# Reordering the first loads of a decoder layer: weight chunk 0 goes between input tiles 1 and 2, chunk 1 between tiles 5 and 6

## The chip, the cores and the metric

The kernel runs on one core of one Trainium2 chip. The metric is the device time of one execution in microseconds (us); lower is better. A kernel's time is the median of several runs.

## What is computed

One post-norm decoder layer on 1024 tokens of width 1024, in float32. The part that matters here is the start of the first sublayer, where all projections read the same input:

```python
def hybrid_mixer(x, w_in, b_forget, conv_w, ...):
    z = x @ w_in                      # x: 1024 x 1024, w_in: 1024 x 4104
    q, k, v, f, glu_a, glu_g, sc_b, sc_c, sc_h = jnp.split(z, IN_SPLITS, axis=-1)
    ...                               # attention, two convolutions, gates, output projection
x = layer_norm(DEEPNORM_ALPHA * x + hybrid_mixer(x, ...), ln1_g, ln1_b)
x = layer_norm(DEEPNORM_ALPHA * x + grouped_moe(x, ...), ln2_g, ln2_b)   # 32 experts, top 2 of one group
```

## The kernel before

Every engine runs its own list of instructions, written out in program order, and waits on semaphores. An engine never passes an instruction that waits, so the order of each list is the order of the work.

**Products in three passes.** A float32 matrix is split into a rounded part `hi` and the rest `lo`; a product is `w_hi*x_hi + w_hi*x_lo + w_lo*x_hi`. ScalarE (ACT) makes each `hi` by a copy, VectorE (DVE) then makes `lo` by a subtraction, and TensorE (PE) multiplies (line 761).

**Input.** `x` comes in eight tiles of 128 tokens, 512 KB each (SyncE, line 393, one semaphore `tile_in[t]` a tile). TensorE transposes a tile with eight 128x128 transposes (line 778, `transpose_in(t)`) into a PSUM bank pair, ScalarE makes `xt_hi` (line 1183), VectorE `xt_lo` (line 1525). Tiles 4 to 7 take over the banks of tiles 1 to 4, so `transpose_in(4..7)` also waits for the VectorE split of tile 1, 2, 3, 4 (`xt_l`).

**Weights.** `w_in` comes in chunks of 512 rows by 128 columns, 256 KB each in pieces of 512 bytes (line 411, `raw(c)`), into a ring of four. Two chunks (the upper and the lower half of the rows) make one output tile of 128 columns by 1024 tokens. ScalarE splits a chunk in line 1179 (`hi_ok`), VectorE in line 1558 (`lo_ok`). `raw(c)` for c of 4 and more waits until the ring's slot is free; the first four wait for nothing.

**The head.** The first output tile is taken in halves, so that TensorE can begin before all of `x` is there: `first_pass(0)`, `(1)` and `(2)` are the three passes of chunk 0 over tokens 0 to 511 (four matmuls each: hi times hi, which waits for all four `xt_hi`; hi times lo, which waits for `xt_l` of 4; lo times hi, which waits for `lo_ok` of chunk 0). Then come `in_mm(1)` for the same tokens (12 matmuls, after chunk 1 is split) and both chunks for tokens 512 to 1023 (24 matmuls, after tile 7 is split). Four small transposes (line 815) follow, and from there the layer's projections run on, chunk after chunk.

The order of the lists before: SyncE issues x 0-3, chunk 0, chunk 1, x 4-7, chunk 2, chunk 3, then small parameters. ScalarE and VectorE split x 0-3, chunk 0, chunk 1, x 4-7, chunk 2 and so on. TensorE does transposes 0-3, `first_pass(0)`, `first_pass(1)`, transpose 4, `first_pass(2)`, transposes 5-7, `in_mm(1)`, the 24 matmuls.

Of the kernel before, what the change touches and what calls it, by code (L numbers as in the profile page):

```python
# [40 lines left out]
TT = SEQ // P  # L41
# [62 lines left out]
def program(nc, x, w_in, b_forget, conv_w, conv_b, conv_ln_g, conv_ln_b, sc_w,  # L104
# [12 lines left out]
    with ctx:  # L117
# [218 lines left out]
        def tiles(b, n=2):  # L336

            return ps[:, b:b + n, :].rearrange("p a (k n) -> p (a k) n", n=P)
# [23 lines left out]
        def x_bank(t):  # L362
            return (0, 2, 4, 6, 2, 4, 6, 2)[t]
# [26 lines left out]
        def _(sp):  # L390

            def load_x(t):
                sp.dma_start(x_raw[:, t, :], x[0, t * P:(t + 1) * P, :]).then_inc(tile_in[t], 16)

            def raw(c):

                if c < CB:
                    kind, half = KINDS[c % NCH // 2], c % 2
                    j = c // NCH
                    src = w_in[0, half * KC * P:(half + 1) * KC * P, j * P + COL[kind]:(j + 1) * P + COL[kind]]  # L400
                elif c < CC:
                    m, half = (c - CB) // 2, c % 2
                    src = w_gate[0, 1 + m // KT, half * KC * P:(half + 1) * KC * P, m % KT * P:(m % KT + 1) * P]
                else:
                    kind, j, half = STREAM[c - CC]
                    if kind == "g":
                        src = w_gate[0, 0, half * KC * P:(half + 1) * KC * P, j * P:(j + 1) * P]
                    else:
                        src = w_branch[0, j // KT, :, j % KT * P:(j % KT + 1) * P]
                sp.wait_ge(lo_ok, c + 1)  # L410
                sp.dma_start(w_raw[:, c % RING], src.rearrange("(k p) n -> p k n", p=P)).then_inc(raw_in[c % RING], 16)
# [12 lines left out]
                    sp.wait_ge(v_t, 2 * i)  # L424
                sp.dma_start(vt_raw[:], qkv_d[2, i * P:(i + 1) * P, :]).then_inc(v_in, 16)

            for t in range(4):
                load_x(t)
            raw(0)
            raw(1)  # L430
            for t in range(4, TT):
                load_x(t)
            raw(2)
            raw(3)
# [38 lines left out]
            for c in range(CC + 4, CE + 6):  # L473
# [10 lines left out]
                t = c - 5 - POS["b", KT, 0] + KT  # L484
# [269 lines left out]
        def _(pe):  # L754
            def product(o, terms, nk, cut, start, stop):


                for k in nk:
                    for n, (st, mv) in enumerate(terms):
                        for h, c0, c1 in cut:  # L760
                            last = nc.tensor.matmul(o(h, c1 - c0), st(k), mv(k, c0, c1),  # L761
                                                    start=start and k == nk[0] and n == 0,
                                                    stop=h in stop and k == nk[-1] and n == len(terms) - 1)
                return last
# [7 lines left out]
            def transpose_in(t):  # L772

                if t >= 4:
                    pe.wait_ge(xt_l, (2, 3, 4, 5)[t - 4])
                pe.wait_ge(tile_in[t], 16)
                for k in range(KT):
                    last = nc.tensor.transpose(tiles(x_bank(t))[:, k, :], x_raw[:, t, k * P:(k + 1) * P], ident[:])
                last.then_inc(xt_t, 1)
# [9 lines left out]
            def first_pass(n):  # L789

                w, v = ((w_hi, xt_hi), (w_hi, xt_lo), (w_lo, xt_hi))[n]
                product(lambda h, _: ps[:, h, :], [(lambda k: w[:, 0, k, :], lambda k, a, b: v[:, k, a:b])],
                        range(KC), HALVES[:1], n == 0, ())
# [6 lines left out]
            first_pass(0)  # L800
            pe.wait_ge(xt_l, 4)
            first_pass(1)
            transpose_in(4)
            pe.wait_ge(lo_ok, 1 + RING)
            first_pass(2)
            for t in range(5, TT):
                transpose_in(t)
            pe.wait_ge(lo_ok, 2 + RING)
# [25 lines left out]
            def scores(n):  # L834

                head, r = n // TT, ORDER[n % TT]
                u, nk, m0 = head % 2, ntiles(r) * P, r * P
                if n % TT == 0:
                    pe.wait_ge(qk_h, 3 * (head + 1))
                    pe.wait_ge(qk_l, 2 * (head + 1))  # L840
                    pe.wait_ge(aug_in[u], 32 * (head // 2 + 1))
                if n >= 2:
                    pe.wait_ge(exp_ok, n - 1)
                else:
                    pe.wait_ge(evac[n], 1 + CT * len(KINDS) // 2)
                out = s_bank(n)
                cut = [(h, a, min(a + HALF, nk)) for h, a in enumerate(range(0, nk, HALF))]
                product(lambda h, w: out[:, h * HALF:h * HALF + w],
                        [(lambda k, q=q: q[u][:, m0:m0 + P], lambda k, a, e, v=v: v[u][:, a:e])
                         for q, v in ((q_dup, k_two), (q_low, k_aug))],  # L850
                        [0], cut, True, [h for h, _, _ in cut if h != m0 // HALF])
                nc.tensor.matmul(out[:, m0:nk], ident_b[:], mask_b[:, 0:nk - m0],  # L852
                                 start=False, stop=True).then_inc(s_ok, 1)
# [34 lines left out]
            def gate_half(n):  # L888

                m, h, j = n // 4, n % 4 // 2, n % 2  # L890
                c = CB + 2 * m + j
                if h == 0:
                    pe.wait_ge(lo_ok, c + 1 + RING)
                if j == 0:
                    pe.wait_ge(tanh_ok, 2 * m + h + 1)
                last = product(lambda _, w: ps[:, 6 + h, :],
                               [(lambda k, w=w: w[:, c % RING, k - j * KC, :], lambda k, a, b, v=v: v[:, k, a:b])
                                for w, v in ((w_hi, xt_hi), (w_hi, xt_lo), (w_lo, xt_hi))],
                               range(j * KC, (j + 1) * KC), (HALVES[h],), j == 0, (h,) if j else ())
                if h == 1:  # L900
                    last.then_inc(w_used, 1)
                elif j == 1:
                    last.then_inc(g_mm, 1)
# [251 lines left out]
        def _(act):  # L1155
# [20 lines left out]
            def split_w(c):  # L1176
                act.wait_ge(raw_in[c % RING], 16 * (c // RING + 1))
                act.wait_ge(w_used, c + 1)
                nc.scalar.activation(w_hi[:, c % RING], w_raw[:, c % RING], ACT.Copy).then_inc(hi_ok, 1)  # L1179

            def split_x_in(t):
                act.wait_ge(xt_t, t + 1)
                nc.scalar.activation(xt_hi[:, :, t * P:(t + 1) * P], tiles(x_bank(t)), ACT.Copy).then_inc(xt_h, 1)  # L1183
# [25 lines left out]
                else:  # L1209
                    nc.scalar.activation(k_aug[u][0:DH, :], k_raw[0:DH, :], ACT.Copy).then_inc(qk_h, 1)  # L1210

            for t in range(4):
                split_x_in(t)
            split_w(0)
            split_w(1)
            for t in range(4, TT):
                split_x_in(t)
            for c in range(2, CB + 2):
                split_w(c)
# [272 lines left out]
        def _(dve):  # L1492
# [29 lines left out]
            def split_x_in(t):  # L1522
                dve.wait_ge(xt_h, t + 1)
                rows_ = slice(t * P, (t + 1) * P)
                nc.vector.tensor_tensor(xt_lo[:, :, rows_], tiles(x_bank(t)), xt_hi[:, :, rows_], ALU.subtract).then_inc(xt_l, 1)  # L1525
# [30 lines left out]
            def split_w(c):  # L1556
                dve.wait_ge(hi_ok, c + 1)
                nc.vector.tensor_tensor(w_lo[:, c % RING], w_raw[:, c % RING], w_hi[:, c % RING], ALU.subtract).then_inc(lo_ok, 1)  # L1558
# [12 lines left out]
                    f_link(nc.vector.tensor_tensor(f_lo[:], fc[:], f_hi[:], ALU.subtract))  # L1571
                    f_link(nc.vector.memset(fc[:], -1.0))

            for t in range(4):
                split_x_in(t)
            split_w(0)
            split_w(1)
            for t in range(4, TT):
                split_x_in(t)
            for i in range(CT):  # L1580
                link = Chain(conv_chain, i * CONV_LINKS)
# [456 lines left out]
```

## Time and profile before

| | |
|---|---|
| Median of 3 runs | 1656.99 us (1656.52 to 1657.79) |
| The profiled execution, its device time | 1657.7 us |
| Its span in the profile | 1656.0 us |
| TensorE busy in the span | 1589.0 us (96%) |
| TensorE's mean granted clock | 0.984 |

The span runs from the first to the last instruction of the profile; the device time holds 1.7 us more, which lie around it. Times in the profile are counted from the start of the span. The layer's first 28.8 us are the head described above; what follows, up to about 1000 us, is the mixer, and the experts stand behind that. "PE" is a matmul or transpose, "PEld" the load of its stationary operand.

### The profile page before, as it was taken

The numbers are of one execution on the slowest core, as the hardware profiler recorded it, in microseconds if no ns is written. First come the engines' busy times: TensorE is split into PE (matmuls) and PEld (weight loads), VectorE is DVE, ScalarE is ACT, GpSimd is POOL, SyncE is SP. The second block draws the span as 40 slices with busy tenths as digits, with TensorE's granted clock in tenths as the row PEclk, the third lists the DMA queues.
The fourth block names the chain that finished last, engine by engine and source line by source line (L and its number), as shares of the span: only waits on it lengthen the run. The fifth ranks groups of instructions, "written<-read, shape, count | busy, mean of one in ns | idle before, by whom it ended". The sixth has DMA issues, their size and how long they took to land.

```text
span 1656.0 us, 20267 instructions
## 1 busy us (share of the span) xinstructions
PE 1589.0 (96%) x7715; PEld 1314.2 (79%) x7715; DVE 1179.1 (71%) x1479; ACT 845.5 (51%) x1176; POOL 185.5 (11%) x219
## 2 busy tenths in 40 slices
PE   8999999999999999999999997999999999999981
PEld 6788888888888888888788885788888888888770
DVE  3756868585666666332575677799999999998884
ACT  3013211215655555325221334688888888888773
POOL 0000000202212220000000001111111111111120
PEclk9999999999999999999999998999999999999995
DMA  5153535644332321411554567999999999999966
GB/s 168 39 106 47 135 68 84 82 93 132 90 103 83 104 84 52 151 47 45 173 174 121 174 219 275 341 378 374 367 361 365 349 361 342 351 353 362 356 228 217
DMA packets 159065, 329.30 MB, mean 199 GB/s; under 512 B 17999, under 2 KB 87631, under 8 KB 158970
## 3 DMA queue, kind: packets, MB, share of 16 engines
q1 hardware_dynamic: 142826, 289.70, 54.1%
q0 software_dynamic: 16144, 38.32, 7.7%
q8 instruction: 61, 1.00, 0.2%
q14 instruction: 34, 0.28, 0.0%
HBM read 296.75 MB, written 48.52 MB: 208 GB/s over the span
## 4 chain that ended last, share of the span: by engine, by line
PE 88%; DMA 6%; DVE 4%; issue 1%; ACT 1%; SPq 0%; DVEq 0%; POOLq 0%; ACTq 0%
PE ps L761 53%; PE ps L1100 26%; DMA e_raw<-in_w_down 3%; PE ps L876 2%; PE ps L861 2%; DVE e_lo L1960 2%; DMA e_raw<-in_w_up 2%; PE ps L1107 1%; PE ps L1041 1%; DMA x_raw<-in_x 1%; PE ps L1113 1%; DVE zout L2020 1%; DVE zout L2013 1%; DMA z_d<-ye,row_i 0%; PE ps L1008 0%
## 5 line engine op out<-in xcount | busy, mean ns | idle before, releaser
L1960 DVE TENSOR_TENSOR e_lo<-e_raw,e_hi 128x1024 fp32r<-128x1024 f32 x376 | 436.1, 1220 | 24.9 <-ACT e_hi L1422 20.6
L1422 ACT ACTIVATE e_hi<-e_raw 128x1024 fp32r<-128x1024 f32 x376 | 367.5, 1050 | 22.2 <-DMA e_raw<-in_w_down 15.8
L761 PE MATMUL ps<-xt_hi,w_hi 128*128 128x512 f32 x896 | 302.3, 394 | 1.7 <-ACT w_hi L1179 1.7
L761 PE MATMUL ps<-xt_hi,w_lo 128*128 128x512 f32 x896 | 298.1, 390 | 0.0
L761 PE MATMUL ps<-xt_lo,w_hi 128*128 128x512 f32 x896 | 298.0, 390 | 0.0
L761 PEld LDWEIGHTS ps<-xt_hi,w_lo 128*128 128x128 f32 x896 | 168.1, 188 | 35.7
L761 PEld LDWEIGHTS ps<-xt_hi,w_hi 128*128 128x128 f32 x896 | 167.8, 188 | 34.7 <-ACT xt_hi L1183 1.9
L761 PEld LDWEIGHTS ps<-xt_lo,w_hi 128*128 128x128 f32 x896 | 168.4, 188 | 33.0 <-DVE xt_lo L1525 0.2
L1558 DVE TENSOR_TENSOR w_lo<-w_raw,w_hi 128x512 fp32r<-128x512 f32 x136 | 95.0, 703 | 131.9 <-ACT w_hi L1179 128.5
L1179 ACT ACTIVATE w_hi<-w_raw 128x512 fp32r<-128x512 f32 x136 | 83.8, 628 | 203.4 <-PE ps L761 195.5
L1100 PE MATMUL ps<-e_hi,xe_hi 128*128 128x512 f32 x512 | 163.6, 401 | 8.5 <-DVE e_lo L1960 7.9
L1100 PE MATMUL ps<-e_lo,xe_hi 128*128 128x512 f32 x512 | 159.6, 393 | 0.0
L1100 PE MATMUL ps<-e_hi,xe_lo 128*128 128x512 f32 x512 | 158.5, 391 | 0.0
L1598 DVE SCALAR_TENSOR_TENSOR conv<-upad,cols,conv 128x1024 f32<-128x1024 f32 x120 | 153.9, 1283 | 3.0
L1100 PEld LDWEIGHTS ps<-e_hi,xe_hi 128*128 128x128 f32 x512 | 92.4, 189 | 27.0 <-issue 8.5
L1100 PEld LDWEIGHTS ps<-e_hi,xe_lo 128*128 128x128 f32 x512 | 96.6, 189 | 21.5
L1100 PEld LDWEIGHTS ps<-e_lo,xe_hi 128*128 128x128 f32 x512 | 96.4, 188 | 21.2
L1245 ACT ACTIVATE pt_hi<-ps 128x1024 fp32r<-128x1024 f32 (+3 forms) x64 | 41.7, 652 | 113.5 <-PE ps L861 113.2
L1606 DVE TENSOR_REDUCE rmax<-ps 128x1 f32<-128x1024 f32 (+3 forms) x64 | 48.4, 756 | 67.7 <-PE ps L852 67.7
L1100 PE MATMUL ps<-e_hi,ht_hi 128*128 128x512 f32 x256 | 82.7, 404 | 3.7 <-DVE ht_lo L1972 3.3
L1100 PE MATMUL ps<-e_lo,ht_hi 128*128 128x512 f32 x256 | 80.1, 395 | 0.0
L1100 PE MATMUL ps<-e_hi,ht_lo 128*128 128x512 f32 x256 | 79.7, 393 | 0.0
(302 smaller groups left out, 2250.0 us busy)
## 6 DMA issues: line engine op xcount, KB each, us to landing
e_raw<-in_w_up SPq DMA_DIRECT2D x128, 1024.0 KB, 21.7
e_raw<-in_w_down SPq DMA_DIRECT2D x64, 1024.0 KB, 21.4
w_raw<-in_w_in SPq DMA_DIRECT2D x64, 256.0 KB, 4.9
w_raw<-in_w_gate SPq DMA_DIRECT2D x48, 256.0 KB, 3.3
gates_d<-gate_t POOLq DMA_DIRECT2D x16, 512.0 KB, 3.3
gate_s<-gates_d SPq DMA_DIRECT2D x16, 512.0 KB, 3.6
qkv_d<-qkv POOLq DMA_DIRECT2D x12, 512.0 KB, 3.7
w_raw<-in_w_branch SPq DMA_DIRECT2D x24, 256.0 KB, 3.7
```

The source lines that it names most:

```text
L761: last = nc.tensor.matmul(o(h, c1 - c0), st(k), mv(k, c0, c1), start=start and k == nk[0] and n == 0, stop=h in stop and k == nk[-1] and n ...
L861: last = nc.tensor.transpose(tiles(4)[:, k, :], prob[n % 2][:, k * P:(k + 1) * P], ident[:])
L876: last = nc.tensor.matmul(o_bank(j), v, p[n % 2][:, k, :], start=k == 0 and s == 0, stop=k == nk - 1 and s == 1)
L1041: last = nc.tensor.matmul(lg, x1t[:, k, :], w_rt[:, k, :], start=False, stop=k == KT - 1)
L1100: last = nc.tensor.matmul(ps[:, banks + h, :], st[:, s, :], w[:, s0 % RSPL, h * HALF:(h + 1) * HALF], start=s == 0 and m == 0, stop=s == n ...
L1179: nc.scalar.activation(w_hi[:, c % RING], w_raw[:, c % RING], ACT.Copy).then_inc(hi_ok, 1)
L1245: nc.scalar.activation(pt_hi[n % 2][:, 0:ntiles(r), (r % 2) * P:(r % 2 + 1) * P], tiles(4)[:, 0:ntiles(r), :], ACT.Copy).then_inc(pt_h, 1)
L1422: nc.scalar.activation(e_hi[:, (UPT + s) % RSPL, :], e_raw[r][:, s % 2, :], ACT.Copy).then_inc(e_h, 1)
L1558: nc.vector.tensor_tensor(w_lo[:, c % RING], w_raw[:, c % RING], w_hi[:, c % RING], ALU.subtract).then_inc(lo_ok, 1)
L1598: link(nc.vector.scalar_tensor_tensor(dst, upad[:, j:j + SEQ], col(ROW_CONVW + j, i), dst, ALU.mult, ALU.add))
L1606: nc.vector.tensor_reduce(rmax[:, n % 2:n % 2 + 1], s_bank(n)[:, 0:ntiles(ORDER[n % TT]) * P], AX.X, ALU.max, negate=True).then_inc(max_ok, 1)
L1960: nc.vector.tensor_tensor(e_lo[:, sp_, :], e_raw[raw_slot(b, s)][:, s % 2, :], e_hi[:, sp_, :], ALU.subtract).then_inc(e_all, 1)
```

## The change

The order of four lists is changed; no instruction is added or removed. SyncE issues x 0-1, chunk 0, x 2-5, chunk 1, x 6-7. ScalarE and VectorE split x 0-2, chunk 0, x 3-5, chunk 1, x 6-7. TensorE does `first_pass(2)` right behind `first_pass(1)`, and transpose 4 after it.

```diff
--- before.py
+++ after.py
@@ -424,11 +424,13 @@
                     sp.wait_ge(v_t, 2 * i)
                 sp.dma_start(vt_raw[:], qkv_d[2, i * P:(i + 1) * P, :]).then_inc(v_in, 16)
 
-            for t in range(4):
+            load_x(0)
+            load_x(1)
+            raw(0)
+            for t in range(2, 6):
                 load_x(t)
-            raw(0)
             raw(1)
-            for t in range(4, TT):
+            for t in range(6, TT):
                 load_x(t)
             raw(2)
             raw(3)
@@ -800,9 +802,9 @@
             first_pass(0)
             pe.wait_ge(xt_l, 4)
             first_pass(1)
-            transpose_in(4)
             pe.wait_ge(lo_ok, 1 + RING)
             first_pass(2)
+            transpose_in(4)
             for t in range(5, TT):
                 transpose_in(t)
             pe.wait_ge(lo_ok, 2 + RING)
@@ -1209,11 +1211,13 @@
                 else:
                     nc.scalar.activation(k_aug[u][0:DH, :], k_raw[0:DH, :], ACT.Copy).then_inc(qk_h, 1)
 
-            for t in range(4):
+            for t in range(3):
                 split_x_in(t)
             split_w(0)
+            for t in range(3, 6):
+                split_x_in(t)
             split_w(1)
-            for t in range(4, TT):
+            for t in range(6, TT):
                 split_x_in(t)
             for c in range(2, CB + 2):
                 split_w(c)
@@ -1571,11 +1575,13 @@
                     f_link(nc.vector.tensor_tensor(f_lo[:], fc[:], f_hi[:], ALU.subtract))
                     f_link(nc.vector.memset(fc[:], -1.0))
 
-            for t in range(4):
+            for t in range(3):
                 split_x_in(t)
             split_w(0)
+            for t in range(3, 6):
+                split_x_in(t)
             split_w(1)
-            for t in range(4, TT):
+            for t in range(6, TT):
                 split_x_in(t)
             for i in range(CT):
                 link = Chain(conv_chain, i * CONV_LINKS)
```

## Rows read from the trace of the kernel before

**Rows 1.** The chain that ended last: start us, us, what it was.

```profile
4.01 11.36 DMA x_raw<-in_x
20.40 8.38 PE ps L761 x36
29.15 349.50 PE ps L761 x1540
```

**Rows 2.** Busy us (instructions) of PE, PEld, DVE, ACT, POOL; clock, DMA share, GB/s.

```profile
0.00:28.80 28.80, 20.82 (x113) 17.25 (x114) 12.01 (x12) 12.84 (x14) 1.64 (x13) 1.00 0.54 189
...
1030.00:1480.00 450.00, 446.40 (x2117) 370.39 (x2116) 418.51 (x440) 366.14 (x420) 66.67 (x49) 1.00 0.98 359
```

**Rows 3.** TensorE in order of time: start us, us, what, [idle before <- releaser].

```profile
12.31 1.16 PE L761 MATMUL ps<-xt_hi,w_hi 128*128 128x512 f32 x4 [1.72 <-ACT w_hi L1179]
13.31 1.09 PE L761 MATMUL ps<-xt_lo,w_hi 128*128 128x512 f32 x4
15.50 1.06 PE L778 MATMUL ps<-ident,x_raw 128*128 128x128 f32 x8 [1.10 <-DMA x_raw<-in_x]
16.32 1.18 PE L761 MATMUL ps<-xt_hi,w_lo 128*128 128x512 f32 x4
17.34 3.06 PE L778 MATMUL ps<-ident,x_raw 128*128 128x128 f32 x24
20.16 0.47 PE L761 MATMUL ps<-xt_hi,w_hi 128*128 128x512 f32 x1
```

**Rows 4.** TensorE between 5.5 and 6.0 us, instructions begun or running then.

```profile
5.25 1.06 PE L778 MATMUL ps<-ident,x_raw 128*128 128x128 f32 x4
```

**Rows 5.** ScalarE (ACT) in order of time.

```profile
11.54 0.62 ACT L1179 ACTIVATE w_hi<-w_raw 128x512 fp32r<-128x512 f32 x1
...
16.60 1.03 ACT L1183 ACTIVATE xt_hi<-ps 128x1024 fp32r<-128x1024 f32 x1 [1.87 <-PE ps L778]
```

**Rows 6.** VectorE (DVE) in order of time.

```profile
9.66 3.49 DVE L1525 TENSOR_TENSOR xt_lo<-ps,xt_hi 128x1024 fp32r<-128x1024 f32 x3 [0.39 <-ACT xt_hi L1183]
13.07 0.68 DVE L1558 TENSOR_TENSOR w_lo<-w_raw,w_hi 128x512 fp32r<-128x512 f32 x1
...
19.47 3.49 DVE L1525 TENSOR_TENSOR xt_lo<-ps,xt_hi 128x1024 fp32r<-128x1024 f32 x3 [0.58 <-ACT xt_hi L1183]
```

**Rows 7.** SyncE issuing the first loads, in order of time.

```profile
0.92 1.82 SPq L393 DMA_DIRECT2D x_raw<-in_x  x4
2.79 1.18 SPq L411 DMA_DIRECT2D w_raw<-in_w_in  x2
```

**Rows 8.** Issue to landing: x 0-1, x 2-3, chunks 0-1, x 4-7, chunks 2-3.

```profile
DMA to landing us min/median/max: 4.0/4.4/4.8
...
DMA to landing us min/median/max: 6.2/6.7/7.1
...
DMA to landing us min/median/max: 7.3/9.0/10.7
...
L393 SPq DMA_DIRECT2D x_raw<-in_x x4: 457/700/1024, 4.0 to 6.3; - x4
...
DMA to landing us min/median/max: 11.4/11.8/12.9
...
L411 SPq DMA_DIRECT2D w_raw<-in_w_in x2: 1072/2033/2994, 7.1 to 8.2; - x2
...
DMA to landing us min/median/max: 13.4/14.6/15.7
```

**Rows 9.** DMA rate between 0 and 30 us, in slices of 0.75 us.

```profile
GB/s 0 0 87 300 251 399 361 284 366 426 360 310 125 55 125 131 236 343 424 426 409 400 382 315 160 118 98 55 30 24 28 32 29 31 16 4 34 48 90 246
```

**Rows 10.** Stretches before and after a fall of the clock; columns as in rows 2.

```profile
8.40:12.30 3.90, 2.14 (x18) 1.68 (x17) 3.51 (x4) 3.48 (x4) 0.00 (x0) 1.00 0.44 146
1044.00:1046.00 2.00, 0.64 (x3) 0.59 (x4) 2.00 (x3) 2.00 (x3) 0.00 (x0) 1.00 0.39 135
1046.00:1050.00 4.00, 4.00 (x12) 3.11 (x11) 4.00 (x5) 3.44 (x4) 0.00 (x0) 0.57 0.64 207
```

## Prediction, made before the changed kernel ran

> **What bounds the kernel now.** I read the chain that ended last first [rows 1]. It goes through the wait for an input tile, then TensorE from 20.40 us on, and from 29.15 us TensorE without a break for 349.50 us. So the change is worth what it moves the end of the head, and the reader should watch one number: E = 20.40 + 8.38 = 28.78 us, where the last of the first two chunks' matmuls ends. Behind E the order is the same. The mixer is TensorE's; in the experts, TensorE is busy 446.40 of 450 us with the DMA engines at a share of 0.98 [rows 2]. Their stream is started by the mixer's end, so I carry a shift of E to the end one to one.
>
> Second, TensorE in order of time [rows 3]. Of 28.8 us it is busy 20.82 [rows 2], so idle 8.0. About 5.0 of them pass before tile 0 has landed, 1.72 in the wait for chunk 0's `w_hi`, 1.10 in the wait for tile 4; the brackets show none from 15.50 on. So only some 3 us of idle time stand behind the first 5.0, and there is a little in the first transposes: four take 1.06 us at 5.25 [rows 4], eight take 1.06 at 15.50 [rows 3]. That stretch ran at the lower clock level, 1.2 GHz against 2.4. The whole head can thus give back some 3 to 4 us at most, if every wait went.
>
> Third, the lists that feed it [rows 5, 6]. VectorE splits a tile in 3.49/3 = 1.16 us and a chunk in 0.68; ScalarE takes 1.03 and 0.62. Fourth, the landings, issue [rows 7] plus time to landing [rows 8]: tiles 0 and 1 at 4.9 and 6.1, tiles 2 and 3 at 8.0 and 9.4, chunk 0 at 2.79 + 7.3 = 10.1, chunk 1 at 3.42 + 10.7 = 14.1, tile 4 at 4.01 + 11.4 = 15.4, tile 7 at 6.3 + 12.9 = 19.2, chunk 2 at 7.1 + 13.4 = 20.5, chunk 3 at 8.2 + 15.7 = 23.9. A tile takes 1.3 us of the stream and, at the same rate, a chunk 0.65. But chunk 1 took 4.0 behind chunk 0, and chunk 3 took 3.4 behind chunk 2; between 9 and 12 us the rate falls to 55 to 131 GB/s [rows 9]. Two chunks in a row starve the stream.
>
> **Part 1, TensorE: `first_pass(2)` ahead of transpose 4.** Chunk 0's `w_lo` was ready at 13.07 + 0.68 = 13.75, but its pass ran at 16.32, behind transpose 4, which waited for its landing. The move fills the 1.10 us of idle time with 0.95 us of work that came later. Alone it would be worth 0.9 to 1.0 us. The cover of tile 4's landing is then this pass.
>
> **Part 2, ScalarE and VectorE: chunk 0 ahead of tile 3.** `first_pass(1)` needs all four `xt_l`. Before, VectorE's run 9.66 + 3.49 = 13.15 ended it, and chunk 0 came after. Now chunk 0's 0.68 stands before tile 3 on VectorE, and its 0.62 before tile 3 on ScalarE, where `first_pass(0)` waits too. The same 0.68 us is on the path that sets the start of the second pass; the third pass no longer needs it.
>
> **Part 3, SyncE: chunk 0 ahead of tiles 2 and 3.** Tiles 0 and 1 are issued as before. Chunk 0 is issued at 1.84, and tiles 2 and 3 land later by what it costs. *Lower bound*: only its bytes, 0.65 us: tile 2 at 8.65, tile 3 at 10.05. *Upper bound*: chunk 1's row, 4.0 us behind tile 1's 6.1, and tiles 1.3 each after it as tile 4 behind chunk 1: chunk 0 at 10.1, tile 2 at 11.4, tile 3 at 12.7. The nearest row is chunk 0 behind tiles (0.7 after tile 3), but it had four tiles to hide behind and now has two, so I take twice the bytes, 1.3 us, an estimate: tile 2 at 9.3, tile 3 at 10.7. Chunk 1 has four tiles ahead of it, as chunk 0 had, and comes at 10.7 + 2.6 + 0.7 = 14.0 at the earliest, up to 19.3 by the 4.0 (15.3 for tile 5). Tile 7 comes by 19.2, since the same ten transfers ended then; up to 21.9 by the upper bound.
>
> **The path to T, the start of transpose 4.** Middle case: tile 2's transposes 9.4 to 10.35, ScalarE tile 2 to 11.5, chunk 0 to 12.15, tile 3 to 13.2; VectorE tile 2 from 11.55 to 12.7, chunk 0 to 13.4, tile 3 to 14.6. Passes two and three take 0.95 to 1.0 each [rows 3], so T = 14.65 + 1.95 = 16.6. With the lower bound VectorE ends tile 3 at 13.95 and T is 15.9. With the upper, tile 3 is transposed by 13.75, copied by 14.9, split by 16.15: T = 18.1. Before, T was 15.50, but with the third pass still ahead, so 16.45 is what to hold it against.
>
> **Part 4, ScalarE and VectorE: chunk 1 behind tile 5.** This one I charge in full. Before, chunk 1 landed at 14.1 and was split while TensorE waited, so `in_mm(1)` began at 20.16 straight behind the transposes. Now its split stands behind tiles 4 and 5, which are not even transposed before T: ScalarE begins tile 4 at T + 1.10 [rows 3, 5], ends it 1.03 later, and VectorE does tile 4, tile 5 and chunk 1 in 1.16 + 1.16 + 0.68 = 3.0. `in_mm(1)` begins at T + 2.15 + 3.0 = T + 5.15. The four tiles' transposes end at T + 4.0 (32 at 3.06/24), so TensorE waits about 1.1 us there. Tiles 6 and 7 are split by T + 7.5, before the 12 matmuls end at T + 7.9, so there is no wait behind them. The 36 matmuls took 28.78 - 20.16 = 8.62 us, with a wait for tile 7, whose split ended only at 22.96 [rows 6]; at 349.50/1540 = 0.227 us each [rows 1] and 0.2 for the end of the last they take 8.35. E = T + 13.5. Chunk 1's landing hides up to T + 3.1, and tile 7's up to E - 9.
>
> **Sum.** Lower bound: 15.9 + 13.5 = 29.4, +0.6 us. Middle: 16.6 + 13.5 = 30.1, **+1.3 us**. Upper: 18.1 + 13.5 = 31.6, +2.8 us. Against the profiled execution's 1657.7 that is 1659.0; the median is 0.7 lower, so the median becomes 1656.99 + 1.3 = **1658.3 us**. 0.2% is 3.3 us, about what a measurement of this kernel can tell from no change, and all three sums lie inside it. Chunks 2 to 5 keep their place: the next matmuls after E need chunk 2, which lands at 20.5.
>
> One rule is weighed against a row here. Chunk 1 landed 4.0 us behind chunk 0, with equal bytes. The Trainium skill, "DMA: Bandwidth & Descriptors", section "Anatomy of one DMA", states for DMAs issued from GpSimd a fixed 2.0 us plus bytes over 436 GB/s, and that many descriptors can be emitted before their cost shows. By it chunk 0 would cost 0.6 us of the stream, and the sum would be the lower bound, +0.6; the 4.0 us of the row speak against it, and the row decides.
>
> **Rivals.**
> *The gap closes.* The reorder gives what part 1 is worth and VectorE's list costs less than I charge: T = 13.15 + 1.95 = 15.1 and `in_mm(1)` follows the transposes at T + 4.7 as before, so E = 15.1 + 13.0 = 28.1 to 28.4, -0.5 us: 1656.5. For it: 1.10 us of idle time really goes. Against it: chunk 0 and chunk 1 both stand in front of splits that gate.
> *TensorE's clock falls in the head, slower.* Between 8.4 and 13.2 us TensorE would have only tiles 2 and 3 to transpose, some 2.1 us in 4.8 (a share of 0.44); before it was 2.14 in 3.90 (0.55), at full clock. In the experts' start it was busy 0.64 of 2.00 us, and the next 4 us were granted 0.57 [rows 10]. If the clock falls to 1.2 GHz there, the three passes and some transposes take twice as long for about such a stretch: +1.7 us more, 1660.0. It decides the sign by 0.2% only with the upper bound of part 3 beneath it: 2.8 + 1.7 = +4.5 us, 1661.5. The Trainium skill, "TensorE: Matmul & The Clock Gate", Part 1, has the idle array at 1.2 GHz and the busy one at 2.4; the trace agrees [rows 4, 10], and by it the time would be this rival's 1660.0.
> *Chunks starve the stream, slower.* As the upper bound, and worse: each chunk costs 4 us where it stands and nothing makes it up. From a landing of tile 3 later than about 13.2, or of tile 7 later than 23, E passes 32.1 and the time 1660.3, slower by over 0.2%. For it: both second chunks cost 3.4 and 4.0. Against it: both came behind another chunk, and here each comes behind tiles.
>
> **How the numbers follow.** The sum from lower to upper bound (1657.6 to 1659.8): 0.63. The gap closes (1656.5): 0.16. The clock falls (about 1660, a third of it beyond 0.2%): 0.12. Chunks starve the stream beyond the bound (over 1660.3): 0.06. More than 3.3 us gained, for which there is no idle time to find: 0.03. Faster 0.03, slower 0.06 + 0.04 = 0.10, within 0.2% 0.87. The range 1656.4 to 1660.2 holds the sum, the gap rival and most of the clock rival; some 0.15 is left out.
>
> **What would show it.** In the changed profile: tile 3's transposes near 10.8 (10.1 to 12.8); no idle time for tile 4 in front of T; VectorE ending tile 3's split near 14.6; `first_pass(1)` waiting for VectorE; T near 16.6; TensorE waiting about 1 us for chunk 1's `w_lo` near 21.7; E near 30.1; the continuous TensorE run after it as long as before. Wrong would be: E below 28.8, a clock under 1.00 between 9 and 25 us, tile 7 landing past 21, or a total that moves by other than E does.

## The result and the profile after

The changed kernel takes 1662.01 us (median of ten, 1660.11 to 1664.68), the kernel before 1657.80 (ten, 1655.97 to 1658.87). The ratio is 1.0028, interval 1.0020 to 1.0036: slower by 0.28%, where I had forecast +0.08%. It is outside the range, and on the side that I had given a chance of 0.10. A second measurement of the changed kernel (e12 below) gave 1.0026 (1.0017 to 1.0035). The forecast started from three executions of the kernel before; the ten lie 0.8 us higher, which is part of the distance to the forecast 1658.3 but not of the ratio. One of the twelve executions of a later experiment, e11, took 6589.92 us, and its ratio leaves that one out.

The chain that ended last in the changed kernel, its first 34 us, as in [rows 1]; start us, us, what:

```profile
2.86 9.37 DMA x_raw<-in_x
...
15.35 4.73 PE ps L763 x12
...
22.05 2.36 DVE xt_lo L1529 x2
24.41 0.61 DVE w_lo L1562
...
25.06 8.45 PE ps L763 x36
```

E, the end of the first two chunks' matmuls, is 25.06 + 8.45 = 33.51 us; before it was 28.78. That is +4.7 us in the profiled execution. The DMA in the first line is tile 3's load. Two later pieces of the same chain:

```profile
33.88 349.50 PE ps L763 x1540
...
804.55 111.81 PE ps L763 x492
```

The second of them in the kernel before:

```profile
799.81 111.81 PE ps L761 x492
```

The first is as long as in [rows 1] and 4.73 us later; the second, near the mixer's end, is as long as before and 4.74 us later. TensorE in order of time, to be held against [rows 3] (this kernel's line 763 is 761 there, 780 is 778):

```profile
11.02 1.10 PE L780 MATMUL ps<-ident,x_raw 128*128 128x128 f32 x8 [2.81 <-DMA x_raw<-in_x]
12.27 1.97 PE L780 MATMUL ps<-ident,x_raw 128*128 128x128 f32 x8 [0.15 <-DMA x_raw<-in_x]
15.35 2.07 PE L763 MATMUL ps<-xt_hi,w_hi 128*128 128x512 f32 x4 [1.11 <-ACT xt_hi L1185]
17.23 1.91 PE L763 MATMUL ps<-xt_lo,w_hi 128*128 128x512 f32 x4
18.93 1.15 PE L763 MATMUL ps<-xt_hi,w_lo 128*128 128x512 f32 x4
19.92 2.78 PE L780 MATMUL ps<-ident,x_raw 128*128 128x128 f32 x24
23.33 1.09 PE L780 MATMUL ps<-ident,x_raw 128*128 128x128 f32 x8 [0.63 <-DVE xt_lo L1529]
25.06 0.50 PE L763 MATMUL ps<-xt_hi,w_hi 128*128 128x512 f32 x1 [0.64 <-DVE w_lo L1562]
```

Two things are to be seen. Tile 2's transposes begin at 11.02, after 2.81 us of idle time, where they followed tile 1's without a gap before. And tile 3's eight transposes take 1.97 us and the first two passes 2.07 and 1.91, where eight transposes took 1.06 before and these passes 1.16 and 1.09 [rows 3]. The windows of the changed kernel, columns as in [rows 2], say why (the last three numbers are clock, DMA share, GB/s):

```profile
8.00:11.00 3.00, 0.21 (x1) 0.00 (x0) 2.04 (x2) 1.02 (x1) 0.00 (x0) 1.00 1.00 406
...
14.00:19.00 5.00, 3.89 (x11) 2.87 (x10) 2.26 (x3) 1.02 (x1) 0.00 (x0) 0.50 0.74 257
```

The granted clock is 0.50 between 14 and 19 us, that is 1.2 GHz, after a stretch in which TensorE was busy 0.21 of 3.00 us. The landings, in the form of [rows 8], for tiles 0-1, chunk 0, tiles 2-5, tiles 6-7:

```profile
L393 SPq DMA_DIRECT2D x_raw<-in_x x2: 397/408/420, 0.9 to 1.4; - x2
...
DMA to landing us min/median/max: 3.5/3.9/4.4
...
L411 SPq DMA_DIRECT2D w_raw<-in_w_in x1: 425/425/425, 1.8 to 1.8; - x1
...
DMA to landing us min/median/max: 7.8/7.8/7.8
...
L393 SPq DMA_DIRECT2D x_raw<-in_x x4: 446/511/2070, 2.3 to 3.9; - x4
...
DMA to landing us min/median/max: 8.7/9.7/10.9
...
L393 SPq DMA_DIRECT2D x_raw<-in_x x2: 512/690/867, 7.1 to 8.0; - x2
...
DMA to landing us min/median/max: 9.8/10.0/10.3
```

Tile 1 lands at 1.4 + 4.4 = 5.8, chunk 0 at 1.84 + 7.8 = 9.7, tile 2 at 2.31 + 8.7 = 11.0, tile 3 at 2.86 + 9.4 = 12.2, tile 7 at 8.0 + 10.3 = 18.3. Chunk 0 lands 3.9 us behind tile 1, and tiles 2 and 3 land 2.9 and 2.8 us later than the 8.0 and 9.4 of before, not 1.3. Yet the ten transfers end at 18.3, not later than the 19.2 of before.

How the chunk costs so much shows in the packets. DMA between 5.2 and 7.5 us, and between 7.5 and 9.7, in the changed kernel:

```profile
DMA packets 416, 0.25 MB, mean 110 GB/s; under 512 B 12, under 2 KB 403, under 8 KB 416
```

```profile
DMA packets 272, 0.85 MB, mean 385 GB/s; under 512 B 23, under 2 KB 71, under 8 KB 272
```

In the first stretch some 390 packets of 512 bytes move at 110 GB/s, and some 13 of 4 KB with them, at a DMA share of 0.53: the DMA engines are idle for nearly half of the stretch, so it is not the moving of the bytes that takes the time. In the second the stream is back at 385 GB/s with 201 packets of 4 KB, all of them of tile 2 and behind (tile 1 had landed at 5.8), and 48 of 512 bytes trickle in between; chunk 0 counts as landed only with the last of them, at 9.7. Tile 2 fares the same. A tile is 128 packets of 4 KB, so tile 2's are among the first 384. Up to its landing at 11.0 some 600 had begun, against some 490 up to its landing at 8.0 in the kernel before:

```profile
DMA packets 1192, 2.72 MB, mean 248 GB/s; under 512 B 80, under 2 KB 592, under 8 KB 1192
```

(1192 less the 592 small ones.) A landing waits for the last piece, while the other pieces of the stream run on. That is how tiles 2 and 3 come later and the last tile does not.

### The profile page after: what moved, and what is told of

It is laid out like the page before. It is cut to its first block, busy times and chain, and to the rows that moved or that the text cites. A ratio compares the mean times of both kernels' runs of the same rounds, so it can differ in the third digit from the quotient of the medians.

```text
span 1660.0 us, 20267 instructions
## 1 busy us (share of the span) xinstructions
PE 1593.6 (96%) x7715; PEld 1317.4 (79%) x7715; DVE 1178.9 (71%) x1479; ACT 845.0 (51%) x1176; POOL 185.8 (11%) x219
## 4 chain that ended last, share of the span: by engine, by line
PE 87%; DMA 6%; DVE 4%; issue 1%; ACT 1%; SPq 0%; DVEq 0%; POOLq 0%; ACTq 0%
PE ps L763 53%; PE ps L1102 26%; DMA e_raw<-in_w_down 3%; PE ps L878 2%; PE ps L863 2%; DVE e_lo L1966 2%; DMA e_raw<-in_w_up 2%; PE ps L1109 1%; PE ps L1043 1%; PE ps L1115 1%; DVE zout L2026 1%; DMA x_raw<-in_x 1%; DVE zout L2019 1%; PE ps L1010 0%; DMA z_d<-ye,row_i 0%
## 5 line engine op out<-in xcount | busy, mean ns | idle before, releaser
L1102 PEld LDWEIGHTS ps<-e_hi,xe_hi 128*128 128x128 f32 x512 | 92.5, 189 | 27.5 <-issue 9.1
L1102 PEld LDWEIGHTS ps<-e_hi,xe_lo 128*128 128x128 f32 x512 | 96.4, 188 | 21.5
## 6 DMA issues: line engine op xcount, KB each, us to landing
e_raw<-in_w_up SPq DMA_DIRECT2D x128, 1024.0 KB, 21.7
```

What stands on the lines that cost most here:

```text
L1102: last = nc.tensor.matmul(ps[:, banks + h, :], st[:, s, :], w[:, s0 % RSPL, h * HALF:(h + 1) * HALF], start=s == 0 and m == 0, stop=s == n ...
```

## The experiments

E is read from each trace's chain; T is the start of transpose 4, as in the prediction. In e2 and e3 TensorE keeps its old list, so the third pass still stands behind T, as in the kernel before (15.5). "Time" is the ratio to the kernel before in the same measurement, with its interval. An execution's time scatters by some 2 us around its median, and a trace's E is that of one execution. The traces of e6 and e8 are of the shortest of their executions, 3.9 and 4.0 us below the medians, so their E may be lower than usual.

| kernel | tile 3 lands | T | E | E against 28.78 | time |
|---|---|---|---|---|---|
| changed | 12.2 | 19.9 | 33.5 | +4.7 | 1.0028 (1.0020 to 1.0036) |
| e1, TensorE's list alone | 8.6 | 15.3 | 28.1 | -0.7 | 1.0000 (0.9991 to 1.0009) |
| e2, SyncE's list alone | 12.6 | 18.6 | 31.8 | +3.0 | 1.0025 (1.0014 to 1.0035) |
| e3, the splits' lists alone | 9.2 | 15.6 | 29.9 | +1.1 | 1.0004 (0.9995 to 1.0013) |
| e11, all but SyncE's list | 9.1 | 16.2 | 29.8 | +1.0 | 1.0004 (0.9995 to 1.0012) |
| e4, kept busy 20 + 12 | 12.5 | 20.5 | 34.2 | +5.4 | 1.0031 (1.0019 to 1.0042) |
| e9, kept busy 9 + 5 | 11.5 | 17.4 | 31.0 | +2.2 | 1.0031 (1.0019 to 1.0042) |
| e5, chunk 0 in 2 KB pieces | 10.7 | 17.5 | 31.1 | +2.3 | one run, 1656.3 us |
| e6, chunk 1 split early | 12.1 | 18.8 | 31.5 | +2.7 | 1.0027 (1.0018 to 1.0037) |
| e7, four tiles first | 9.0 | 15.7 | 28.9 | +0.1 | 1.0002 (0.9994 to 1.0011) |
| e8, chunks on a second queue | 12.3 | 19.2 | 32.0 | +3.2 | 1.0031 (1.0022 to 1.0041) |
| e10, chunk 0 ahead of all | 12.4 | 19.4 | 32.1 | +3.4 | 1.0020 (1.0012 to 1.0029) |
| e12, changed again | 13.0 | 21.5 | 35.2 | +6.4 | 1.0026 (1.0017 to 1.0035) |
| e13, kept busy 12 + 5 | 11.7 | 19.7 | 33.3 | +4.6 | 1.0019 (1.0010 to 1.0028) |
| e14, kept busy 9 + 5 again | 12.9 | 18.9 | 32.5 | +3.7 | one run, 1661.4 us |
| e15, changed, third trace | 12.4 | 20.5 | 34.1 | +5.4 | one run, 1662.8 us |

(Tile 0 landed between 4.4 and 4.9 in these traces, 4.9 in the kernel before; e10's landed at 8.4.)

**One list at a time.** e1 is the kernel before with

```diff
-            transpose_in(4)
             pe.wait_ge(lo_ok, 1 + RING)
             first_pass(2)
+            transpose_in(4)
```

> The kernel before with one edit: first_pass(2) ahead of transpose 4. E is the end of the first two chunks' matmuls, 28.78 us before. By part 1 of the prediction the pass fills the 1.10 us wait for tile 4, so E is 27.8 to 27.9 and the time 0.9 to 1.0 us less. The rival, read only now: tile 7 lands at 19.2 and its transposes began at 19.34, so the landing holds the transposes, the 36 matmuls begin at 20.2 either way and E stays at 28.7 to 28.9, time unchanged.

The rival holds. TensorE's rows of e1:

```profile
14.41 1.09 PE L761 MATMUL ps<-xt_hi,w_lo 128*128 128x512 f32 x4
15.34 1.98 PE L778 MATMUL ps<-ident,x_raw 128*128 128x128 f32 x16
17.54 1.06 PE L778 MATMUL ps<-ident,x_raw 128*128 128x128 f32 x8 [0.22 <-DMA x_raw<-in_x]
18.84 1.07 PE L778 MATMUL ps<-ident,x_raw 128*128 128x128 f32 x8 [0.23 <-DVE xt_lo L1525]
```

The pass runs at 14.41, the 1.10 us gap is gone, and TensorE then waits for tiles 6 and 7 as they land. Tiles 0 and 7 landed 0.5 us sooner in this trace, and E is 0.7 sooner. Counted from tile 7's landing, E comes after 28.11 - 18.70 = 9.4 us, before after 28.78 - 19.20 = 9.6. So part 1 of the prediction is worth at most some 0.2 us by itself; the time (1.0000, with 0.0009 on either side) could not tell 1 us from nothing.

e2 takes over only SyncE's part of the diff, e3 only the two split lists, e11 everything except SyncE's part.

> The kernel before with SyncE's new order alone (x 0-1, chunk 0, x 2-5, chunk 1, x 6-7); the splits and TensorE keep the old order. If the landings carry the loss, tile 2 lands near 11.0 and tile 3 near 12.3 as in the changed kernel, TensorE's clock falls to 1.2 GHz in the wait too, and E is 30.4 at full clock, 31.5 to 32.5 with the fall, +1.6 to +3.7 us. If the order of the splits carries it (rival), E stays below 29.5.

> The kernel before with the new order of ScalarE's and VectorE's splits alone; loads and TensorE as before. By parts 2 and 4 of the prediction the second pass waits 0.7 us longer and chunk 1's split behind tile 5 delays the 12 matmuls to about 21.4: E 29.8 to 30.0, +1.0 to +1.3 us, at full clock throughout. If the landings alone carry the loss (rival), E is 28.7 to 29.0 and the time unchanged.

> The changed kernel with SyncE's order of before (x 0-3, chunk 0, chunk 1, x 4-7): the new splits and the new place of first_pass(2) alone. By the prediction's parts 1, 2 and 4 with full-rate landings T is 15.5 to 15.9 and E 29.2 to 29.6, +0.5 to +0.9 us; what is left to the changed kernel's 33.4 is then SyncE's order with the fallen clock, 3.9 to 4.2 us. If the three lists only lose together (rival), E is 31 or more.

e2 has nearly the whole loss in the time (0.25 of 0.28%), with tile 2 landing at 11.3 and tile 3 at 12.6; of E it has 3.0 of the 4.7. The clock fell in it too, but only for the transposes of tiles 2 and 3 (16 in 3.58 us); its passes ran at full pace. e3 and e11 have E at 29.9 and 29.8, with all passes at full pace. e3's wait, which part 4 of the prediction charged:

```profile
17.41 3.08 PE L778 MATMUL ps<-ident,x_raw 128*128 128x128 f32 x24
21.42 0.50 PE L761 MATMUL ps<-xt_hi,w_hi 128*128 128x512 f32 x1 [0.92 <-DVE w_lo L1560]
```

The 12 matmuls begin at 21.42 behind chunk 1's `w_lo`, where I had written "about 21.4". T in e3 is 15.6 against 15.5 before, since tile 4's landing at 15.4 holds it in both; so the 1.1 us are part 4's, and part 2 costs nothing there. The lists of the splits cost 1.0 to 1.1 us of E and SyncE's list the rest. The times add up in the same way: 0.25% for e2 and 0.04% for e11, 0.28% for the changed kernel.

**What a chunk costs.** e5 reads chunk 0 as 128 rows of 2 KB in place of 512 pieces of 512 bytes. It leaves out the right weights of chunk 0, so that the first output tile holds other numbers:

```diff
+                if c == 0:
+                    sp.dma_start(w_raw[:, 0].rearrange("p k n -> p (k n)"), w_in[0, 0:P, 0:KC * P]).then_inc(raw_in[0], 16)
+                    return
```

> The changed kernel, but chunk 0 is read as 128 rows of 2 KB in place of 512 pieces of 512 bytes: the same 256 KB in a quarter of the pieces. It leaves out the right weights: chunk 0 holds other numbers of w_in, so the first output tile is another. If the number of pieces is what costs, chunk 0 lands 0.7 to 1.3 us behind tile 1 (near 6.8), tile 2 at 8.3 to 8.8, tile 3 at 9.6 to 10.1, and E is 29.4 to 30.2. If the bytes or the place in the list cost (rival), chunk 0 lands near 9.6 and tile 2 near 11.0 as in the changed kernel.

```profile
L412 SPq DMA_DIRECT2D w_raw<-in_w_in x1: 422/422/422, 1.8 to 1.8; - x1
...
DMA to landing us min/median/max: 6.3/6.3/6.3
```

Chunk 0 lands at 1.84 + 6.3 = 8.1, 2.1 us behind tile 1. With 512 pieces it was 3.9, 4.6 and 3.9 in the three traces of the changed kernel, and 3.1 to 4.6 in the kept-busy ones (below), whose loads are the same. So the size of the pieces carries a part of it, by one trace; but 2.1 is not the 0.65 us of the bytes, and neither side of the expectation had it.

e7, e10 and e8 move chunk 0 to where it might be cheap: SyncE's order x 0-3, chunk 0, x 4-5, chunk 1, x 6-7; chunk 0 ahead of all tiles (and split behind tile 1); both chunks issued by ScalarE. All three have `first_pass(2)` ahead of transpose 4.

> The kernel before with SyncE's order x 0-3, chunk 0, x 4-5, chunk 1, x 6-7 and first_pass(2) ahead of transpose 4; the splits as before. If a chunk starves the stream only where fewer than about three tiles stand ahead of it, chunk 0 lands at 10.1 as before, tile 4 at 11.4 to 12 in place of 15.4, tile 7 at 17 to 18.5, T is 15.3 to 15.5 and E 28.0 to 28.4: 0.4 to 0.8 us faster than before. If the total of pieces sets the landings (rival), tile 7 lands at 18.8 to 19.2 and E is 28.4 to 28.8, time unchanged.

> The kernel before with chunk 0 issued ahead of all tiles (order chunk 0, x 0-3, chunk 1, x 4-7), split between tiles 1 and 2, and first_pass(2) ahead of transpose 4. If what costs is a chunk without several tiles ahead of it, the pieces of chunk 0 take 3.5 to 4 us alone, tile 0 lands at 6.5 to 8.5 and everything behind it is 2 to 3 us late: E 30 to 31.5. If the loss belongs to the place between tiles only (rival), tile 0 lands at 5.6, 0.65 us later than before, tile 7 near 19, and E is 28.2 to 29.

> The kernel before with chunks 0 and 1 issued by ScalarE at its start in place of SyncE, the eight tiles in a row on SyncE, and first_pass(2) ahead of transpose 4. If the pieces of a chunk hold up only what stands behind them in the same queue, tiles 4 to 7 land at 11.5, 12.8, 14.1 and 15.4 or so, tile 3 at 9.4 to 10.7, T is 15.3 to 16.6 and E 28.0 to 29.3 with tile 7 no longer waited for: -0.8 to +0.5 us. If both queues share what is short (rival), tile 2 lands at 11 as in the changed kernel, the clock falls and E is 31 or more.

The landing of chunk 0 in e7, issued at the same 2.79 as before and behind the same four tiles:

```profile
DMA to landing us min/median/max: 9.2/9.2/9.2
```

It takes 9.2 us, so it lands at 12.0, where [rows 8] had 7.3 and 10.1. Only what is issued behind it differs: a tile in e7, another chunk before. So the 10.1 was no sign that a chunk behind four tiles is cheap. Alone it lands 12.0 - 9.0 = 3.0 us behind tile 3; the pair's second chunk landed 14.1 - 9.4 = 4.7 behind it, and that is where the pair's cost showed. Nothing is gained in e7: tile 7 lands at 19.4, E is 28.9, the time the same. In e10 chunk 0, first in the queue, takes 6.2 us, tile 0 lands at 8.4 and tile 3 at 12.4: the loss of the first theory, a little larger (E 32.1). In e8 a second queue does not help; its DMA up to 12 us, by queue (packets, MB, share of 16 engines):

```profile
q1 hardware_dynamic: 712, 2.62, 58.7%
q10 hardware_dynamic: 1024, 0.51, 16.5%
```

The chunks' 1024 packets run on a queue of their own, and yet tile 1 lands at 8.5 in place of 5.8 and tile 2 at 10.9. What is short is shared by both queues. ScalarE issued the chunks at 1.1 and 1.6 us, though, beside the first tiles; chunks issued later on that queue were not tried. In all seventeen traces, the kernel before's too, tile 7 lands between 17.4 and 19.4.

**The clock.** e4, e9, e13 and e14 are the changed kernel with extra transposes of the identity, into a bank that nobody reads. The diff is e4's; e9 and e14 have 9 and 5 in place of 20 and 12, e13 has 12 and 5.

```diff
+            def keep_busy(n):
+
+                for _ in range(n):
+                    nc.tensor.transpose(ps[:, 1, 0:P], ident[:], ident[:])
 
             for t in range(4):
                 transpose_in(t)
+                if t == 1:
+                    pe.wait_ge(xt_l, 1)
+                    keep_busy(20)
+            keep_busy(12)
```

> The changed kernel, with 20 extra transposes of the identity after tile 1 and 12 after tile 3, into a PSUM bank that nobody reads; they fill TensorE's waits and change no result. If the fallen clock costs what the trace suggests, the clock stays at 1.00 in the head, transpose 4 begins at 18.2 to 18.5 in place of 19.9, E is 31.7 to 32.0 in place of 33.5, and the time is 1.5 to 1.8 us less than the changed kernel's: +2.5 to +3 us against before. If the clock is beside the point (rival), E stays at 33.3 or more, or the extra work makes it later.

> The changed kernel with 9 extra transposes of the identity after tile 1 and 5 after tile 3, into a bank that nobody reads. The run with 20 and 12 held the clock at 1.00, but the extra transposes took 0.21 us each and made tile 2's transposes begin 2.2 us after its landing; 9 take 1.9 us and fit the wait. If the fallen clock costs the changed kernel 1.7 us on top of the late landings, transpose 4 begins at 17.9 to 18.5, E is 31.4 to 32.0, the time +2.5 to +3 us against before. If the clock is worth nothing here (rival), E stays near 33.4.

e4 failed as a test: its extra work ran until 13.4, 2.2 us past tile 2's landing. e9 in TensorE's rows:

```profile
9.02 1.21 PE L800 MATMUL ps<-ident 128*128 128x128 f32 x9 [0.67 <-DVE xt_lo L1538]
...
11.52 1.09 PE L780 MATMUL ps<-ident,x_raw 128*128 128x128 f32 x8 [0.19 <-DMA x_raw<-in_x]
...
13.88 1.19 PE L763 MATMUL ps<-xt_hi,w_hi 128*128 128x512 f32 x4 [0.72 <-ACT xt_hi L1194]
15.44 1.20 PE L763 MATMUL ps<-xt_lo,w_hi 128*128 128x512 f32 x4 [0.37 <-DVE xt_lo L1538]
...
17.39 2.78 PE L780 MATMUL ps<-ident,x_raw 128*128 128x128 f32 x24
...
22.52 0.50 PE L763 MATMUL ps<-xt_hi,w_hi 128*128 128x512 f32 x1 [0.63 <-DVE w_lo L1571]
```

Tile 3's transposes take 1.09 us again, the passes 1.0; T is 17.39 and E 31.0. But its time over six executions was no better than the changed kernel's, and the trace came from one of the fastest of them. So I ran the changed kernel twice more and two kept-busy versions, to see whether the traces are typical.

> The changed kernel once more, beside a kept-busy version on the same chip. Its first trace has tile 3 landing at 12.2, the clock at 1.2 GHz from 12.2 to 19.0 and E 33.4. If that trace is typical, this one has the clock fallen in the head too and E 32.5 to 34; if the fall is an accident of one execution (rival), E is 31.5 or less at full clock while the time stays about +4.5 us, and the clock is not the cause.

> A third trace of the changed kernel. Tile 2 lands at 10.8 to 11.3 and tile 3 at 12.0 to 12.6 if the landings are steady; the clock falls once or twice between 10.9 and 19; E 32.5 to 34.

> The version with 9 and 5 extra transposes once more, for a second trace of its head: its first came from one of the fastest of its executions. E 31 to 32.2 at full clock if the first was typical; 32.5 or more with tile 3 landing after 12.3 if it was not.

> The changed kernel with 12 extra transposes of the identity after tile 1 and 5 after tile 3. If the fallen clock costs 1.7 us in most executions, E is 31 to 32 and the time 1.5 to 2 us below the changed kernel's of the same call. If in most executions the late landings alone set the time (rival), both take the same.

e12 in windows, columns as in [rows 2]:

```profile
8.00:10.80 2.80, 0.00 (x0) 0.00 (x0) 2.18 (x2) 1.02 (x1) 0.00 (x0) 1.00 0.92 371
11.00:21.00 10.00, 8.12 (x27) 6.75 (x28) 2.96 (x3) 2.56 (x3) 0.00 (x0) 0.50 0.73 264
```

All three traces of the changed kernel run tile 3's transposes and the first two passes at half pace. In two of them the clock had been up before and fell; in the third no instruction before 19.5 us shows the full pace. Landings scatter, so the measure is the time from tile 3's landing to E: 33.5 - 12.2 = 21.3, 35.2 - 13.0 = 22.2 and 34.1 - 12.4 = 21.7 in the changed kernel; 31.0 - 11.5 = 19.5 and 32.5 - 12.9 = 19.6 in e9 and e14, which differ from it only in the extra transposes. By these the low clock costs 2.2 us of E.

It does not cost that in every execution. e6, the last experiment below, has the changed kernel's loads, its list for TensorE and its splits up to tile 3's, and the same wait of 2.8 us:

```profile
10.83 3.61 PE L780 MATMUL ps<-ident,x_raw 128*128 128x128 f32 x16 [2.82 <-DMA x_raw<-in_x]
15.55 1.20 PE L763 MATMUL ps<-xt_hi,w_hi 128*128 128x512 f32 x4 [1.11 <-ACT xt_hi L1185]
16.84 1.20 PE L763 MATMUL ps<-xt_lo,w_hi 128*128 128x512 f32 x4
```

The transposes ran at half pace and the passes at full pace. From tile 3's landing at 12.1 to T it took 6.7 us, against 7.7, 8.5 and 8.1 in the three traces of the changed kernel and 5.9 in e9 and e14: there the clock cost 0.8 us.

e13's twelve ran at half pace themselves, 2.82 us, and made tile 2 wait 1.3 us, so its E is 33.3. In the time the clock's part does not come out. e13 and e12 were measured together, with medians of 1661.09 and 1661.15 and ratios 1.0019 and 1.0026 whose intervals overlap, and e9 takes 1.0031. The mean clock over each kernel's executions differs: 0.9819 and 0.9823 for the changed kernel (10 and 11 executions), 0.9837, 0.9835 and 0.9842 for e4, e9 and e13, and 0.9834 to 0.9837 for the kernel before (24 and 26). So the extra transposes do raise the granted clock; that this shortens an execution is shown by E in two traces and by no time.

**Chunk 1's place.** e6 is the changed kernel with `split_w(1)` directly behind `split_x_in(3)` in both lists.

> The changed kernel with chunk 1's split ahead of tile 4's on ScalarE and VectorE. By part 4 of the prediction the place behind tile 5 costs TensorE some 1.1 us (0.63 + 0.64 of waits in the changed kernel's trace): the 36 matmuls begin at T + 4.5 in place of T + 5.15, some of it given back in a wait for tile 7's split, so E - T is 13.0 to 13.3 in place of 13.6, the time 0.3 to 0.6 us less than the changed kernel's. If part 4 costs nothing (rival), E - T stays at 13.6.

```profile
18.78 2.78 PE L780 MATMUL ps<-ident,x_raw 128*128 128x128 f32 x24
22.20 1.09 PE L780 MATMUL ps<-ident,x_raw 128*128 128x128 f32 x8 [0.63 <-DVE xt_lo L1528]
23.05 0.48 PE L763 MATMUL ps<-xt_hi,w_hi 128*128 128x512 f32 x1
```

The 36 matmuls begin at T + 4.27 without a wait for `w_lo`; E - T is 12.7 in place of 13.6. It is worth 0.9 us, more than expected, and drowns in the time, where e6 takes what the changed kernel takes.

No version with the right weights beats the kernel before.

## Why the prediction was wrong

**The step that failed first is a term of part 3.** I took 1.3 us for what chunk 0 costs tiles 2 and 3, and gave 4.0 us behind tile 1 as the upper bound. Tile 3 landed at 12.2, 13.0 and 12.4 in place of 10.7, so the term measured 2.8 to 3.5 us (it was 9.4 before), and chunk 0 landed 3.9 to 4.6 us behind tile 1. I had chosen by the row of chunk 0 behind four tiles, and read the dip behind it as the fault of "two chunks in a row". e7 shows that reading wrong: the same chunk behind the same four tiles lands 1.9 us later when tiles follow. The pair's cost stood on chunk 1, and a single chunk has its own (3.0 us in e7), so the bound should have been the value.

The rule that I weighed there, of the Trainium skill's "DMA: Bandwidth & Descriptors", "Anatomy of one DMA", would have given less still (0.6 us). The page gives it for another issuing engine. Neither its fixed cost plus bytes nor descriptors whose cost shows late fits the 110 GB/s and e5's 2.1 us.

**The clock rival came true, on top.** I gave it 0.12, priced it at 1.7 us and let it cross 0.2% only with the upper bound of part 3 beneath it: "2.8 + 1.7 = +4.5 us". Both happened; E went up by 4.7 in the profiled execution. My error was to hold the two apart: it is the late landing of tile 2 that empties TensorE's stretch (0.21 us busy of 3.00 between 8 and 11). The low clock measured 2.2 us of E in the three traces of the changed kernel and 0.8 in e6's.

**How the miss divides.** E was forecast at 30.1 and is 34.3 in the mean of the three traces. Of these 4.2 us, 1.8 are tile 3's later landing (12.5 in the mean, for 10.7) and 2.2 the clock. What is left is 0.1.

**What stood.** From tile 3's landing at 10.7 I had worked out T = 16.6, 5.9 us later; at full clock it is 17.39 - 11.47 = 5.9 (e9) and 18.86 - 12.93 = 5.9 (e14). E - T was forecast at 13.5 and is 13.6 in the changed kernel. The lower bound, 29.4, had tile 3 at 10.05; e11, with the old landings, has 29.8. e3 has +1.1 where I had expected 1.0 to 1.3. Part 1, "alone it would be worth 0.9 to 1.0 us", was wrong: tile 7's landing was next in line (e1). That did not enter the sum, since T and E - T were worked out whole. The rival "the gap closes" has a slip: its T + 4.7 "as before" counts the third pass, which there stands ahead of T. By the prediction's own T + 4.0 its E would be about 27.5, which tile 7's landing at 19.2 would not have allowed.

**Where the shift of E lies, by mean of the traces.** Splits and TensorE's list: e11's E less the one of before, 1.0. SyncE's list at full clock: the mean of e9 and e14 (31.7) less e11, 2.0. The clock: the mean of the changed kernel's three (34.3) less 31.7, 2.6, of which 0.3 are later landings in those executions. Together, unrounded, 5.5. The two terms of SyncE's list rest on two and three traces.

**From E to the end.** The mixer passes the shift on to the hundredth, as the two later pieces of the chain show. The measured time moved by 0.26 to 0.28%, 4.3 to 4.6 us, and E by 5.5 in the mean of three. The span less E is 1627.2 us before and 1626.5, 1624.2 and 1627.1 in the three traces of the changed kernel (their spans are 1660.0, 1659.3 and 1661.2); in the other experiments with the right weights it is 1624.7 to 1630.0. The expert stage scatters that much from one execution to the next. Whether it gives back some of the shift, these runs don't settle.

## What to carry to other kernels

A load in many small pieces should be charged at what it costs a transfer that stands behind it and is waited for; where two such loads stand in a row, the cost of both shows on the second. Moving one forward trades an early arrival for a later one of what stands right behind it, while the last transfer of the group lands at about the same time (17.4 to 19.4 us in every order tried here). And a longer wait in front of TensorE is to be priced with the clock that falls in it: here each of the five traces with the wait of 2.7 to 3.8 us left empty has slow instructions behind it, though what they cost differs from one execution to the next (0.8 to 2.6 us up to T, by the changed kernel's traces and e6's against 5.9). The two are one event, not two chances.

## What the runs showed of the hardware

The granted clock of the profile can read 1.00 where TensorE's pace says 1.2 GHz. In the third trace of the changed kernel the windows and TensorE's rows are

```profile
11.00:13.00 2.00, 1.85 (x9) 1.85 (x10) 0.00 (x0) 0.00 (x0) 0.00 (x0) 1.00 1.03 394
16.00:19.00 3.00, 3.00 (x7) 2.41 (x8) 1.17 (x2) 0.00 (x0) 0.00 (x0) 1.00 0.54 159
```

```profile
11.15 3.67 PE L780 MATMUL ps<-ident,x_raw 128*128 128x128 f32 x16 [2.74 <-DMA x_raw<-in_x]
...
17.80 1.91 PE L763 MATMUL ps<-xt_lo,w_hi 128*128 128x512 f32 x4
19.51 1.17 PE L763 MATMUL ps<-xt_hi,w_lo 128*128 128x512 f32 x4
```

The clock column reads 1.00 in both windows. Yet the 16 transposes take 3.67 us, where eight take 1.09 at full pace, and the four matmuls of the second pass 1.91, where the four behind them take 1.17. The same holds for the first transposes of every trace (16 in 3.65 us here). The pace of equal instructions is the safer witness, and the mean clocks above miss such stretches. The second surprise is that a queue of its own did not free the tiles from the chunks: with the chunks' 1024 packets on another queue, tile 1 landed 2.7 us later than with four tiles ahead of them in one queue (8.5 in e8, 5.8 in e7).
